# Gate products and row spreadings woven into the scan mixer's projection units, and a bias added as two part products

## What is computed

```python
def chunked_sgu(u, v, w_s, b_s):
    v = v.reshape(B, n_chunk, SGU_CHUNK, SGU_GROUPS, SGU_GROUP_DIM)
    mixed = jnp.einsum('gts,bnsgc->bntgc', w, v) + b_s.T[None, None, :, :, None]
    return u * mixed.reshape(B, S, SGU_WIDTH)
# token_mix: p = h @ w_in; a_out = chunked_sgu(gelu(u), gelu(va), w, b); b_out = top-k attention(q, k, v)
```

```python
u = rms_norm_2(x, mix_norm[l]) @ w_in[l]
lru_x, lru_g, mq, mk, mv, cq = jnp.split(u, split_at, axis=-1)
xb = causal_depthwise_conv(lru_x, lru_conv_w[l], lru_conv_b[l])
# rg_lru(xb):
r = sigmoid(xb @ block_diagonal(a_w) + a_b);  i = sigmoid(xb @ block_diagonal(x_w) + x_b)
log_a = -8 * r * softplus(-lam);  a = exp(log_a);  mult = sqrt(-expm1(2 * log_a))
h_t = a_t * h_{t-1} + mult_t * i_t * xb_t
y_lru = h_lru * gelu(lru_g)
q, k, qc, kc = rms_norm_2 of each head, then the attentions
x = x + concat([y_lru, y_moba, y_mem]) @ w_out[l]
```

## Time and profile before

| | |
|---|---|
| median of 3 runs | 2897.14 us (2895.5 to 2900.47) |
| the profiled execution, its own time | 2895.73 us |
| its span, first to last instruction | 2894.0 us, mean granted clock 0.996 |
| busy: PE / DVE / ACT / POOL | 2862.3 (99%) / 1586.1 (55%) / 869.5 (30%) / 292.0 (10%) us |
| chain that ended last | PE 89%, DVE 4%, issue 3%, each other engine 1% or less |
| DMA | 351.26 MB, mean 121 GB/s |

### The profile page before, as it was taken

How to read it: one execution, slowest core, us unless ns; L and a number is a source line. 1 busy time by engine, 2 the same in 40 slices (tenths; PEclk the granted TensorE clock), 3 DMA queues, 4 the chain that set the end, 5 groups by cost and what they waited for, 6 DMA issues and landing times.

```text
span 2894.0 us, 36100 instructions
## 1 busy us (share of the span) xinstructions
PE 2862.3 (99%) x13875; PEld 2365.1 (82%) x13875; DVE 1586.1 (55%) x2257; ACT 869.5 (30%) x1026; POOL 292.0 (10%) x152
## 2 busy tenths in 40 slices
PE   8999999999999999999999999999999999999999
PEld 6888887888888888887887888888888878788887
DVE  7654658776524565366687762364433556753232
ACT  3222233453222322123335421243212244532121
POOL 0000005340000200000462200000000024100000
PEclk9999999999999999999999999999999999999999
DMA  6544532125523255353321462322322321223221
GB/s 264 200 160 148 191 111 83 60 73 197 203 73 106 98 174 203 109 189 121 112 67 62 169 217 94 105 102 84 108 82 101 116 89 45 74 99 119 73 99 75
DMA packets 63759, 351.26 MB, mean 121 GB/s; under 512 B 7842, under 2 KB 10274, under 8 KB 36260
## 3 DMA queue, kind: packets, MB, share of 16 engines
q1 hardware_dynamic: 62564, 347.90, 33.9%
q10 hardware_dynamic: 1088, 1.97, 0.4%
HBM read 345.78 MB, written 2.10 MB: 120 GB/s over the span
## 4 chain that ended last, share of the span: by engine, by line
PE 89%; DVE 4%; issue 3%; DVEq 1%; POOL 1%; ACT 1%; POOLq 1%; DMA 0%; SPq 0%; ACTq 0%
PE bank L320 29%; PE bank L322 28%; PE bank L321 28%; DVE m_m L1679 1%; DVEq L1678 1%; PE bank L328 1%; PE bank L1285 1%; PE bank L1262 1%; POOLq L540 0%; POOL m_wL L261 0%; DVE m_masks L1687 0%; DVE m_mod_big L2290 0%; DMA m_mod_big<-in_ada_w 0%; PE bank L1271 0%; POOL m_pw L542 0%
## 5 line engine op out<-in xcount | busy, mean ns | idle before, releaser
L320 PE MATMUL bank<-m_hH,m_wH 128*128 128x512 f32 x2464 | 968.1, 393 | 8.7 <-DVE m_wL L285 6.3
L322 PE MATMUL bank<-m_hH,m_wL 128*128 128x512 f32 x2464 | 961.2, 390 | 0.0
L321 PE MATMUL bank<-m_hL,m_wH 128*128 128x512 f32 x2464 | 960.8, 390 | 0.0
L285 DVE TENSOR_TENSOR m_wL<-m_wraw,m_wH 128x2048 fp32r<-128x2048 f32 (+3 forms) x185 | 461.4, 2494 | 551.9 <-ACT m_wH L292 551.3
L292 ACT ACTIVATE m_wH<-m_wraw 128x2048 fp32r<-128x2048 f32 (+3 forms) x233 | 454.1, 1949 | 883.0 <-PE bank L322 879.4
L320 PEld LDWEIGHTS bank<-m_hH,m_wH 128*128 128x128 f32 x2464 | 464.0, 188 | 107.4 <-issue 12.8
L322 PEld LDWEIGHTS bank<-m_hH,m_wL 128*128 128x128 f32 x2464 | 463.7, 188 | 97.3
L321 PEld LDWEIGHTS bank<-m_hL,m_wH 128*128 128x128 f32 x2464 | 464.0, 188 | 94.3 <-issue 0.2
L320 PE MATMUL bank<-m_guH,m_wH 128*128 128x512 f32 x1248 | 491.6, 394 | 3.2 <-DVE m_x L1354 2.8
L322 PE MATMUL bank<-m_guH,m_wL 128*128 128x512 f32 x1248 | 485.9, 389 | 0.0
L321 PE MATMUL bank<-m_guL,m_wH 128*128 128x512 f32 x1248 | 485.8, 389 | 0.0
(11 more groups left out here) (294 smaller groups left out, 2132.4 us busy)
## 6 DMA issues: line engine op xcount, KB each, us to landing
m_wraw<-in_ffn_in SPq DMA_DIRECT2D x132, 1024.0 KB, 4.8
m_mod_w<-in_ada_w SPq DMA_DIRECT2D x144, 512.0 KB, 4.5
m_wraw<-in_ffn_out_a SPq DMA_DIRECT2D x24, 1536.0 KB, 8.2
m_wraw<-in_ffn_out_b SPq DMA_DIRECT2D x24, 1280.0 KB, 5.8
m_wraw<-in_mix SPq DMA_DIRECT2D x30, 1024.0 KB, 4.8
m_wraw<-in_mix SPq DMA_DIRECT2D x26, 512.0 KB, 3.7
m_mod_big<-in_ada_w SPq DMA_DIRECT2D x16, 512.0 KB, 11.8
m_x<-in_x SPq DMA_DIRECT2D x2, 1024.0 KB, 6.4
```

The source lines that it names most:

```text
L285: nc.vector.tensor_tensor(m.wL[:, j, 0:size], m.wraw[:, j, 0:size], f(m.wH[:, j, 0:size]), ALU.subtract).then_inc(s.low, 1)
L320: nc.tensor.matmul(out, a[0], b[0], start=first, stop=False)
L321: nc.tensor.matmul(out, a[0], b[1], start=False, stop=False)
L322: return nc.tensor.matmul(out, a[1], b[0], start=False, stop=last)
```

## The change

Three edits, and a table of ones in fp32r for the second of them.

1. In `Mix2.pe` the gate products stand in three lots, 0 to 2, 3 to 5, and 6 and 7, with the first half of unit 3 (bank 2) behind the first lot and the second half (bank 3) behind the second. `Mix2.act` and `Mix2.dve` are as they were.
2. In `Mix1.pe` each bias product in fp32 becomes two in fp32r, of a high and a low part of the bias, which POOL makes on one partition behind the mask (a copy, a drain, a subtraction).
3. In `Mix2.pe` four groups of unit 7 go ahead of each of the spreadings 4 to 7 (`pe_rows_part`), so 16 of its 32 groups lie within unit 6, and with them the wait for unit 7's weights and for the eviction of unit 5.

```diff
-        for n in range(8):
-            pe.wait_ge(s.xb, n % 4 + 1)
-            if n >= 3:
-                pe.wait_ge(s.sgm, n - 2)
-            nc.tensor.matmul(m.bank[5 + n % 3][:], m.gatew[:, n // 4, n % 4], m.xb[:, n % 4], start=True, stop=True)\
-                .then_inc(s.ga, 1)
-        proj.pe_tiles(pe, nc, s, 3)
+
+        def gates(some):
+            for n in some:
+                pe.wait_ge(s.xb, n % 4 + 1)
+                if n >= 3:
+                    pe.wait_ge(s.sgm, n - 2)
+                nc.tensor.matmul(m.bank[5 + n % 3][:], m.gatew[:, n // 4, n % 4], m.xb[:, n % 4], start=True, stop=True)\
+                    .then_inc(s.ga, 1)
+        gates(range(0, 3))
+        proj.pe_part(pe, nc, s, 3, range(0, KD))
+        gates(range(3, 6))
+        proj.pe_part(pe, nc, s, 3, range(KD, 2 * KD))
+        gates(range(6, 8))
...
         for r in range(self.CHAIN):
             proj.pe_part(pe, nc, s, 6, range(2 * r, 2 * r + 2))
+            if r >= self.CHAIN // 2:
+                at = 4 * (r - self.CHAIN // 2)
+                proj.pe_rows_part(pe, nc, s, 7, range(at, at + 4))
             spread(r)
-        proj.pe_rows(pe, nc, s, 7)
+        proj.pe_rows_part(pe, nc, s, 7, range(2 * self.CHAIN, TT * KD))
...
+    def pe_rows_part(self, pe, nc, s, n, groups):
+
+        if groups[0] == 0:
+            pe.wait_ge(s.low, self.u0 + n + 3)
+            self.banks(pe, s, n)
+        for g in groups:
+            tt, k = divmod(g, KD)
...
                 if c == 0:
-                    nc.tensor.matmul(m.bank[4 + g][:], m.ones[0:1, :], m.sgub[0:1, g].unsqueeze(1).to_broadcast([1, TT, P]),
-                                     start=True, stop=False)
+                    for part in (m.sgubH, m.sgubL):
+                        nc.tensor.matmul(m.bank[4 + g][:], m.ones_r[0:1, :], part[0:1, g].unsqueeze(1).to_broadcast([1, TT, P]),
+                                         start=part is m.sgubH, stop=False)
...
-                                base=0, channel_multiplier=-1).then_inc(s.sgw, 1)
+                                base=0, channel_multiplier=-1)
+        nc.gpsimd.tensor_copy(m.sgubH[0:1], m.sgub[0:1])
+        pool.drain()
+        nc.gpsimd.tensor_tensor(m.sgubL[0:1], m.sgub[0:1], f(m.sgubH[0:1]), ALU.subtract).then_inc(s.sgw, 1)
```

More of the change, by code:

```diff
@@ L177, in memory @@
     m.sgub = at("sgub", a + 10 * K, [4, P])
+    m.sgubH = at("sgubH", a, [4, P], F32R)
+    m.sgubL = at("sgubL", a + 2 * K, [4, P], F32R)
     m.memk = at("memk", a, [2, 256])
@@ L210, in memory @@
     m.warm = small("warm", [P], F32R)
+    m.ones_r = small("ones_r", [P], F32R)
     m.gains = small("gains", [LAYERS, 3 * KD])
@@ L1464, in pe_part @@
                 mm.then_inc(s.mm, 1)
+    def pe_rows_part(self, pe, nc, s, n, groups):
[4 more added lines that the diff above has]
+            tt, k = divmod(g, KD)
+            hi, lo = self.h(k)
+            w = [x[:, n % 2, k * COLS:(k + 1) * COLS] for x in (self.m.wH, self.m.wL)]
+            out = self.m.bank[2 * (n % 2) + tt // 2][:, tt % 2 * COLS:(tt % 2 + 1) * COLS]
+            mm = pe_3(nc, out, (hi[:, tt * P:(tt + 1) * P], lo[:, tt * P:(tt + 1) * P]), w, k == 0, k == KD - 1)
+            if tt % 2 == 1 and k == KD - 1:
+                mm.then_inc(s.mm, 1)
     def pe_rows(self, pe, nc, s, n):
@@ L2300, in dve @@
         dve.drain()
+        nc.vector.tensor_copy(m.ones_r[:], m.ones[:])
         nc.vector.tensor_copy(m.warm[:], m.ident).then_inc(self.ms, 1)
```

## The result

The changed kernel took 2901.7 us (median of 20 runs, 2899.06 to 2904.01) where the kernel before took 2897.26 (20 runs, 2895.09 to 2901.77): a ratio of 1.0013, 95% interval 1.0007 to 1.0019. That is 4.4 us, slower than before by a measurable amount and less than the 0.2% that counted here as a change. The forecast was 2899.0, range 2892 to 2904.

What follows compares the result with a forecast made beforehand. PE was busy 99% of the span, but at the mixers other engines were taken to be late. Scan's mixer +1.6 and first block +0.3 made +1.9: 2895.73 to 2897.6 us, as a median 2899.0, range 2892 to 2904.

Steps and rivals of the forecast that it cites:

- 0.45 us a group: First block's bias: PE saves 0.45 us in each of four groups, 3.6 in all, hidden behind DVE, worth 0.
- delay booked at +0.3: First block: POOL's two new bias instructions delay the first index products, +0.3 us for two layers, bounds 0 and 2.
- last sigmoid: Scan's mixer, ACT: product 6 runs behind unit 3, so the last sigmoid ends 7.8 us later.
- second stopped operation: Scan's mixer, DVE: one more stop beside POOL's low part of unit 6, 4.0 us; `m_hv` starts 6.3 us later.
- stall of 4.85 us ahead of spreading 0: Scan's mixer: PE waits 4.2 us for ACT's broadcast, and the spreadings start 1.8 us later than before.
- forecast stall of 2 us: Scan's mixer: PE stands another 2 us for POOL's low part of unit 7.
- spacing of the spreadings: Scan's mixer: spreadings 4 to 7 spaced by 1.44 us more, taken as 0.7 us more to the last gated tile.
- third normalization: Scan's mixer, DVE: it waits for POOL's first low part of the tiles and comes 3.2 us later.
- The attention: Scan's mixer: the attention's first group waits for the last gated tile, +1.6 us, bounds -1 and +4.5.
- rival (c): PE's clock falls behind longer waits ahead of the three attentions, +5.1 us on top of +1.9: 2904; chance 0.15.
- Rival (a): PE's own account holds, 3.1 and 2.1 us reach the end: 2892, or 2888 with the bias paid out; chance 0.16.
- rival (b): No net shift: one DVE stop of 4 us is lost, `m_hv` starts near 2415.5, total 2896; chance 0.17.

Runs made afterwards that it cites:

- early statistics: The changed kernel with DVE's head statistics and their Newton step moved behind the recurrence's second column: 2898.45 us, ratio to the kernel before 1.0000.
- all fillers: The changed kernel plus unused matmuls of ones ahead of both first-block attentions, spreading 0 and the second block's first projection group: 2900.28 us, 1.0005 to before.
- gates alone: The kernel before with only the first edit, gate products in three lots between halves of unit 3: 2901.51 us, ratio 1.0010.
- long weave: Any kernel with the change's first edit, half of unit 3 behind each of the first two gate lots; as the only edit to the kernel before, 2901.51 us.
- first-block ones: The changed kernel plus eight unused matmuls of ones ahead of the two first-block attentions only: 2899.18 us, ratio to the kernel before 1.0003.
- both weaves: The changed kernel with one fp32 product for each bias, as before: 2899.82 us, ratio to the kernel before 1.0003.
- short weave with rows: The kernel before with unit 7 woven and only five groups of unit 3 ahead of the fourth gate product: 2892.76 us, ratio 0.9981.

## Why the prediction was right, and where it was short

**Bias.** 0.45 us a group was forecast, 0.40 measured, and that it is hidden held: in the first layer the last split ends 133.58 us behind the first index eviction, before 133.72. The delay booked at +0.3 was not there. POOL's two instructions took 0.60 and 1.54 us and made the first index product 0.8 us late, but DVE's long chain did not move, and in the second layer it was 0.7 shorter. What I left out of the sum is the clock: the wait grew from 0.79 to 1.97 and 1.69 us, the clock fell behind both, and each fall cost 1.6 us. Net of the table: +1.43 and +0.84. So the term that fell short here is the bias and its delay, +0.3 with bounds 0 and 2: it measured +2.3, of which 3.2 are the two falls and -0.9 the earlier end of DVE's chain, by 0.1 and 0.7.

**Gate products.** Step by step nearly as written: head sums 3.3 us earlier (3.1 forecast), last sigmoid +7.65 (+7.8), the second stopped operation and with it `m_hv` +6.33 (+6.3), stall of 4.85 us ahead of spreading 0 (4.2). This is the mechanism of the change and no luck of the sum, since each step was read from its own row. The early statistics show that this chain, and not POOL or the gated tiles, set the spreadings. I expected 0.8 us of stall for unit 5's low part; it was 0.2.

**Unit 7.** POOL began its low part at +56.40, where I had 56.4. The forecast stall of 2 us ahead of unit 7's first group is absent: the clock at 1.2 GHz had made PE itself late, and in the kernel with all fillers, which had no fall there, it was 0.28 us. The step that failed is the spacing of the spreadings: I let PE run on from spreading 0 at full pace, but spreading 2 waits for a broadcast that stands on ACT behind a table load, two evictions and the high part of unit 7, and PE with it (1.30 us in the profile of the gates alone). For the sum this step did not matter, because DVE was the later one: the third normalization came at +3.5 to +3.7 in the three profiles without the long fall (+3.2 forecast) and at +5.3 in the changed kernel's. From there to the last gated tile DVE took 17.0 us in all four, as before, where I had 17.8. How the long fall reached DVE is in the rows: it put the second normalization at 56.3 us behind the first gate product in place of 54.2 to 55.1, so that the product behind it (L1969) began after POOL's start at 56.4 and took 4.42 us. In the other three it began ahead of POOL and took 0.69, and an operation behind it stood instead (4.7 to 4.9 us), so DVE was one operation further when POOL ended. The attention: +1.1 to +1.2 without the long fall (forecast +1.6; the lower figure is worked out from the gated tile where fillers held PE), +2.84 with it.

**Sum and rivals.** Forecast +1.9: scan's mixer 1.6, first block 0.3. Measured in the pair of traces: 2.8 and 2.3, together 5.1. The other 1.6 of the 6.7 us lie in stages that no edit touches: falls of the clock at 1362 and 1601 us, which before's profile does not have, made them 1.1 us longer each (1.07 and 1.12), and the start of the first mixer was 0.6 earlier. By the medians, 2899.0 was 2.7 us below the 2901.7 measured. The mechanism was right, and the missing term is the clock of rival (c), in part: of the three attentions that it named the clock fell at two, 1.6 us each, and held at the third behind a wait of 2.09 us; the long fall of 1.6 came at spreading 0, which it had not named. Without these three falls the two terms would have measured about +1.2 and -0.9, where 1.6 and 0.3 stood. So that the forecast lies as near as it does is in part luck: terms somewhat too large stood in for the clock. Rival (c) was given 0.15 because the clock had held behind a stall of 3.04 us; the other profiles that kept this stall show it falling there, three of three. One execution was no ground for a chance that low. The edits alone add up to +2.4 by their medians (+3.3, +1.6, -2.5), the whole to +4.4; the difference is about what two series differ by, and is not explained. Rival (a) is refuted by the gates alone, rival (b) by `m_hv`, which stands at 49.3 in all five profiles with the long weave and the statistics in their old place.

What stays open: whether the run with all fillers is slower at all than that with the first-block ones. Its median is 1.1 us higher, but the runs overlap (2897.06 to 2902.93 and 2896.3 to 2901.33); between the two profiles lie 0.6 us at the attention, from surplus matmuls, and 0.9 in the second layer, where the two kernels are the same. And no run shows how often the clock falls at each place, only that it did in one execution of each kernel.

## What to carry to other kernels

A stall filled with work is won only as far as nothing in a chain of the other engines stands behind that work: put in as much as the wait is long (five groups of 0.68 us for 3.04), and keep the producers of a long chain in their old place in time. Saving time on PE where another engine is late makes its wait longer, and the clock may then take more than was saved. Ask of a late chain also what merely stands behind it in an engine's order: moving five small instructions was worth as much (3.3 us) as the weave had cost (3.3).

## What the runs showed of the hardware

A fall of TensorE's clock to 1.2 GHz between the first mixer and the scan's attention lasted 3.4 or 6.8 us in every profile. One of 3.4 cost 1.6 us behind the start of the first block's attentions and 1.6 to 1.7 at the gate products, 1.1 us in the stage at 1600 us (799.0 us from the second mixer to the gate products without it, 800.05 with it), near nothing where another engine was later than PE. At the start of the first block's attentions it came behind each wait of 1.7 to 2.2 us (six of six in the three kernels with the bias and no filler) and behind none of 0.8 us (five kernels without the bias edit, two layers each). This is no rule for other places: at the first projection group of the scan's attention it fell behind waits of 2.11 and 2.12 us (both weaves, early statistics) and held behind two of 2.09 (changed, short weave with rows). Four profiles of the long weave show a fall 33 us behind the first gate product, where PE had just done 16 head sums of two columns and then waited 0.16 us. POOL's instructions of one partition and 512 elements took 0.60 us (copy) and 1.54 us (subtraction); two subtractions on 128 partitions take 3.18, so the partitions that stand empty save nothing.
